# S5's parameter work beside the branch input products, and its gate tiles in two blocks instead of three

## The chip, the core and the metric

One core of a Trainium2 chip. The metric is the device time of one execution in microseconds, lower is better. Engines: TensorE (PE; PEld is its weight load), VectorE (DVE), ScalarE (ACT), GpSimd (POOL), and SyncE (SP), which here only issues DMA transfers.

## The reference

A first block (two layers of Fourier, pooling and latent attention) gives h; a second block, one layer, mixes four branches of 256 channels: S5, forgetting attention, RWKV and stick-breaking attention. Sequence 1024, width 1024. What the change touches is the S5 branch, a state space model of 16 groups with 16 channels and 64 complex states each:

```python
proj = h @ w_in[i]
(s5_u, fq, fk, fv, ff, rw, sq, sk, sv, gates) = _split(proj, IN_SPLIT_SIZES)
# _s5_mixer
dt = jnp.exp(log_dt)[:, None]
mag = jnp.exp(lam_re * dt); ang = lam_im * dt
lb_re = mag * jnp.cos(ang); lb_im = mag * jnp.sin(ang)
den = jnp.square(lam_re) + jnp.square(lam_im); nr = lb_re - 1.0
f_re = (nr * lam_re + lb_im * lam_im) / den
f_im = (lb_im * lam_re - nr * lam_im) / den
bb_re, bb_im = f * b          # complex product, per group
bu = ug @ bb                  # inputs of the states
x = associative_scan(x[t] = lb * x[t-1] + bu[t])
y = Re(c @ x) + d * ug
y = jax.nn.gelu(y); y = y * jax.nn.sigmoid(y @ glu_w + glu_b)
# later
merged = sum(sigmoid(gates[:, :, n]) * (branches[n] @ w_branch[i, n]) for n in range(4))
```

The gates are a part of the same projection: 4096 columns, 32 tiles of 128.

## The kernel before

Channels lie on the 128 partitions, positions along the free axis. A product in float32 is made from two parts of each operand (hi and lo), three products of fp32r matmuls: hi·hi, hi·lo, lo·hi. Weights come in tiles of 1024 x 128 (512 KB) through class `Weights`: `load` (SP, DMA into `w_raw`, two buffers; tile g waits for the split of tile g-2), `split` (GpSimd: a cast to `w_hi`, L197, and a subtract to `w_lo`, L201; waits for the end of tile g-2's products), and the products on TensorE.

**Branch input products** (`branch_products`, L608). 23 tiles (`N_PROJ2`) of the projection, 48 matmuls of 128x512 each, two PSUM accumulators in turn. VectorE reads each tile into `stage` times the row norm (L458, L460; L448 for the two S5 tiles, 8 and 9, which it writes by position within a chunk of 8), ScalarE's queue issues the store to `proj2` in HBM. For tiles 0 to 7 VectorE also norms a row of h.

**Gate tiles** (`GateTiles`, L673). They fill TensorE in the branches behind. A tile is two halves of 512 positions, 24 matmuls each (L696), with two PSUM banks once `gates.two` is set. VectorE reads each half into `gate_stage` (L723), SP stores it to `gates_kept` (L734, L736). A block says how many pieces (`gates.tensor(pe, n)`, 8 pieces to a half), reads, stores and splits it takes, at fixed places in each engine's program, which runs in order. Of a half, bank x may be begun when half x-2 was read; a read waits for the store of half x-2.

**S5** (`s5_branch`, L2493, and `s5_states`, L2783) has three parts in two blocks:
1. Parameters (6 gate tiles). SP loads the parameters, the masks, `glu`, and u from `proj2` in two layouts (2 rows and 16 rearranged pieces). VectorE makes dt, angles, coefficients, powers of lambda (`pw`), shift powers (`aw`) and the output matrices `hout`, in chains of small operations; ScalarE makes Exp and Sin; GpSimd clears `toe` and the pads of the scan and makes `fin` with six wide operations. The 12 gate reads stand between them.
2. States, in the same hardware block (6 gate tiles). TensorE transposes `fin`, makes the local states from u and the Toeplitz rows from `hout` and `bb`; SP spreads these into `toe` with 8 transfers; VectorE runs the scan over 128 chunks: 7 steps of 32 shifts (L2865) with a gate read after 16 of them; then TensorE has only gate halves.
3. Outputs, in a block of its own (2 gate tiles). TensorE: output products (L2740, L2742), 2 gate halves, wait for Gelu, GLU product (L2750), 2 gate halves. Between them results go to HBM and come back in another layout.

A hardware block ends when all engines are through; the row after it shows `PEq`, `POOLq` as what ended the wait. At each block's end SP clears the semaphores of the block before it. The RWKV branch follows.

Of the kernel before, what the change touches and what calls it, by code (L numbers as in the profile page):

```python
# [15 lines left out]

# [11 lines left out]
P = 128  # L28
# [584 lines left out]
def branch_products(core, io, hi, lo, stage, sq, h_all, vecs, r, ones, coming, comes_first):  # L613
# [6 lines left out]
    with core.phase(*x.SEMAPHORES, "stored0", "stored1", "h_normed", "h_stored", "next_in") as (block, *sems):  # L620
        stored0, stored1, h_normed, h_stored, next_in = sems[len(x.SEMAPHORES):]
# [757 lines left out]
def second_block(core, io, h_all, h_life, ones, ident, final_w, r, comes_first):  # L1379
# [3 lines left out]
    with core.scope():  # L1383
        vecs = core.sb("vecs2", [P, int(V_END)])
        right = ExitStack()
        with core.scope():
            h_at = 122880
            hi, lo = (rows_of(core.place("h2", [P, KT, T2], h_at + n * 4 * KT * T2, FR)) for n in range(2))
            with core.scope():
                stage, last_sq = core.sb("stage", [P, 2, T2]), core.sb("last_square", [P, TP])  # L1390
                branch_products(core, io, hi, lo, stage, last_sq[:], h_all, final_w, r, ones, [(vecs[:], io["vec2"])],
# [6 lines left out]
            with core.scope():  # L1398
                s5_branch(core, io, gates, masks, vecs, ybr, [(masks[:], io["masks"])])
# [1093 lines left out]
def s5_branch(core, io, gates, masks, vecs, ybr, coming):  # L2493
# [3 lines left out]
    nc = core.nc  # L2497
    par = core.sb("s5_par", [P, 3, 8])
    bc = core.sb("s5_bc", [P, 4, 8, S5_CH])
    tmp = core.sb("s5_tmp", [P, 16, 8])  # L2500
    rnd = core.sb("s5_round", [P, 8], I32)
    pw = core.sb("s5_powers", [P, 2, SC + 1, 8])
    aw = core.sb("s5_shift_powers", [P, 3, 7, 8])
    bb = core.sb("s5_bbar", [P, 3, 8, S5_CH])
    fin = core.sb("s5_in", [P, 2, 8, P])
    finT = ybr[:, BR_S5:BR_S5 + 2, :].rearrange("p a (t n) -> p a t n", t=8)
    hout = core.sb("s5_out", [P, 2, S5_G, (SC + 1) * S5_CH])
    toe = core.sb("s5_toeplitz", [P, S5_G, P])
    u = core.sb("s5_u", [P, 2, T2])
    ug = core.sb("s5_ug", [P, S5_G, NCH])  # L2510
    glu = core.sb("s5_glu", [P, 2, 2, P])
    ks = [ybr[:, 2 + 3 * n:5 + 3 * n, :].rearrange("p a t -> p (a t)")
          .rearrange("p (q t n) -> p q t n", q=2, t=8) for n in range(2)]
    kt = core.sb("s5_scan_tmp", [P, 2, 2, T2])
    lre, lim, ldt = (par[:, i, :] for i in range(3))
    (dt, mag, ang, turns, sn, sh, den, nr, fre, fim, t1, t2, t3, rdn, _, _) = (tmp[:, i, :] for i in range(16))
    PI = 3.1415925

    def cmul(tt, out_re, out_im, ar, ai, br, bi, p, q):

        tt(p, ar, br, ALU.mult)
# [6 lines left out]

    gates.two = True
    loads = 16 * (3 + len(coming) + 2 * SC)  # L2530
    with core.phase("p_dve", "p_exp", "p_ang", "p_sin", "p_ready", "p_pool", "p_out", "p_in", "par_in", "bc_in",
                    "rest_in") as \
            (block, stepped, exp_ready, ang_ready, sin_ready, par_ready, pool_step, hout_ready, fin_ready, par_in,
             bc_in, rest_in):
        @block.sync
        def _(sp):
            sp.dma_start(par[:], io["s5_par"]).then_inc(par_in, 16)
            sp.dma_start(bc[:], io["s5_bc"]).then_inc(bc_in, 16)
            sp.dma_start(glu[:], io["s5_glu_w"]).then_inc(rest_in, 16)
            for dst, source in coming:  # L2540
                sp.dma_start(dst, source).then_inc(rest_in, 16)
            for m in range(2):
                sp.dma_start(u[:, m, :], io["proj2"][P_S5 + m]).then_inc(rest_in, 16)
                for i in range(SC):
                    sp.dma_start(ug[S5_CH * i:S5_CH * (i + 1), 8 * m:8 * m + 8, :],
                                 io["proj2"][P_S5 + m].rearrange("(g c) (i n) -> i c g n", g=8, i=SC)[i]) \
                        .then_inc(rest_in, 16)
            gates.sync(sp, 6)

        @block.tensor  # L2550
        def _(pe):
            gates.tensor(pe, 12 * KT)

        @block.scalar
        def _(act):
            link = chain(act, exp_ready)
            act.wait_ge(par_in, 16)
            link(nc.scalar.activation(dt, ldt, ACT.Exp))
            act.wait_ge(ang_ready, 1)
            link(nc.scalar.activation(mag, mag, ACT.Exp))  # L2560
            nc.scalar.activation(sn, ang, ACT.Sin).then_inc(sin_ready, 1)
            nc.scalar.activation(sh, ang, ACT.Sin, scale=0.5).then_inc(sin_ready, 1)

        @block.vector
        def _(dve):
            link = chain(dve, stepped)

            def tt(o, a, b_, op):
                link(nc.vector.tensor_tensor(o, a, b_, op))

            def ts(o, a, s1, s2, op0, op1=ALU.bypass):
                link(nc.vector.tensor_scalar(o, a, s1, s2, op0, op1) if s2 is not None
                     else nc.vector.tensor_scalar(o, a, s1, None, op0))
            dve.wait_ge(exp_ready, 1)
            tt(mag, lre, dt, ALU.mult)
            tt(ang, lim, dt, ALU.mult)

            ts(turns, ang, 1.0 / (2 * np.pi), None, ALU.mult)
            link(nc.vector.tensor_copy(rnd[:], turns))
            link(nc.vector.tensor_copy(turns, rnd[:]))  # L2580
            for part in (6.28125, 0.0019350051879882812, 3.0199159819999247e-07):
                ts(t1, turns, part, None, ALU.mult)
                tt(ang, ang, t1, ALU.subtract)
            link(nc.vector.tensor_scalar(ang, ang, PI, -PI, ALU.min, ALU.max))
            nc.vector.tensor_copy(t1, ang).then_inc(ang_ready, 1)
            for _half in range(2):
                gates.vector(dve)
            dve.wait_ge(sin_ready, 2)
            dve.wait_ge(exp_ready, 2)
            tt(t1, sh, sh, ALU.mult)  # L2590
            ts(t1, t1, -2.0, 1.0, ALU.mult, ALU.add)
            lbr, lbi = pw[:, 0, 1, :], pw[:, 1, 1, :]
            tt(lbr, mag, t1, ALU.mult)
            tt(lbi, mag, sn, ALU.mult)
            tt(t1, lre, lre, ALU.mult)
            tt(t2, lim, lim, ALU.mult)
            tt(den, t1, t2, ALU.add)
            link(nc.vector.reciprocal(rdn, den))
            ts(nr, lbr, 1.0, None, ALU.subtract)
# [12 lines left out]
            dve.wait_ge(bc_in, 16)
            tt(bb[:, 0], wide(fre), bc[:, 0], ALU.mult)
            tt(bb[:, 2], wide(fim), bc[:, 1], ALU.mult)
            tt(bb[:, 0], bb[:, 0], bb[:, 2], ALU.subtract)
            tt(bb[:, 1], wide(fre), bc[:, 1], ALU.mult)
            tt(bb[:, 2], wide(fim), bc[:, 0], ALU.mult)
            tt(bb[:, 1], bb[:, 1], bb[:, 2], ALU.add)
            gates.vector(dve)

            link(nc.vector.memset(pw[:, 0, 0, :], 1.0))
# [1532 lines left out]
```

## Time and profile before

| | us |
|---|---|
| median of 3 runs | 3381.97 |
| lowest, highest | 3373.53, 3384.65 |
| span of the profiled execution | 3381.1 |

The profiled execution's device time isn't given apart from its span. The page of the profile shows TensorE busy for 95% of the span, VectorE for 61%, ScalarE 30%, GpSimd 29%. A timeline row gives start, duration, engine, line, operation, tiles and count; in brackets the idle time before it and what ended it. Ends of matmuls are modelled, so idle times of TensorE are a little short; starts are exact. A row of the waits says: engine and line, for whom it waited, total us, times, longest.

### The profile page before, as it was taken

Reading aid. Unit: us, or ns where it says so; the run is one execution under the profiler, and the core shown is the slowest. Engines: PE = TensorE matmul, PEld = TensorE weight load, DVE = VectorE, ACT = ScalarE, POOL = GpSimd, SP = SyncE. Lnnn points to the kernel's source line nnn. Section 1 sums busy time; section 2 is a strip of 40 time slices with the busy share of each in tenths; the row PEclk is TensorE's granted clock in tenths of the full one; section 3 lists DMA queues with packets and bytes.
Section 4 is the critical chain, followed back from the end, with each engine's and each line's share of the span. In section 5 each row is a group of like instructions: output and inputs, shape, how many; then the busy total and the mean of one; then the engine's idle time right before and its main releaser. Section 6 shows DMA issues by size and latency. Waiting matters only on the chain. (4 is left out here: it accounts for less than half of the span.)

```text
span 3381.1 us, 41800 instructions
## 1 busy us (share of the span) xinstructions
PE 3200.5 (95%) x17082; PEld 2723.7 (81%) x17082; DVE 2047.7 (61%) x2416; ACT 1009.5 (30%) x1456; POOL 967.0 (29%) x623
## 2 busy tenths in 40 slices
PE   7998999999899999998888999999999999999997
PEld 7997888999688898877767996666677787888875
DVE  5635664444466544118856554655686766896788
ACT  2113332101233320001022221455432644344644
POOL 3320001333000023334323322100132443445575
PEclk9999999999999999999989999999999999999998
DMA  3120000211100013233241002311261454355443
GB/s 134 44 64 9 21 1 19 77 44 44 33 29 1 7 45 143 101 104 95 83 146 57 1 1 92 86 44 35 97 237 58 140 180 160 119 189 170 149 158 120
DMA packets 111758, 282.12 MB, mean 83 GB/s; under 512 B 15010, under 2 KB 20770, under 8 KB 111552
## 3 DMA queue, kind: packets, MB, share of 16 engines
q1 hardware_dynamic: 107104, 263.19, 23.9%
q10 hardware_dynamic: 4464, 16.25, 1.2%
q8 instruction: 136, 2.23, 0.3%
q14 instruction: 54, 0.44, 0.0%
HBM read 237.37 MB, written 41.42 MB: 82 GB/s over the span
## 5 line engine op out<-in xcount | busy, mean ns | idle before, releaser
L197 POOL CAST w_hi<-w_raw 128x1024 fp32r<-128x1024 f32 x116 | 136.8, 1179 | 1780.7 <-PE psum L210 1112.6
L3595 PE MATMUL psum<-x,w_hi 128*128 128x512 f32 x2016 | 626.0, 392 | 8.3 <-DVE x L3566 3.2
L3595 PEld LDWEIGHTS psum<-x,w_hi 128*128 128x128 f32 x2016 | 378.4, 188 | 93.0 <-issue 6.9
L3595 PE MATMUL psum<-x,w_lo 128*128 128x512 f32 x1008 | 393.0, 390 | 0.0
L696 PE MATMUL psum<-h,w_hi 128*128 128x512 f32 x1024 | 331.8, 406 | 31.2 <-DVE gate_stage L723 17.8
L3480 POOL TENSOR_TENSOR w_lo<-w_sum,w_hi 128x512 fp32r<-128x512 f32 x180 | 251.9, 1407 | 331.2 <-ACT w_hi L3474 331.2
L201 POOL TENSOR_TENSOR w_lo<-w_raw,w_hi 128x1024 fp32r<-128x1024 f32 x116 | 302.8, 2610 | 16.4 <-DVE y L1501 7.2
L696 PEld LDWEIGHTS psum<-h,w_hi 128*128 128x128 f32 x1024 | 190.8, 193 | 83.5 <-issue 25.5
L3595 PEld LDWEIGHTS psum<-x,w_lo 128*128 128x128 f32 x1008 | 189.6, 188 | 39.6
L210 PE MATMUL psum<-hn_hi,w_hi 128*128 128x348 f32 x864 | 189.0, 327 | 17.7 <-DVE hn_lo L407 16.2
L696 PE MATMUL psum<-h,w_lo 128*128 128x512 f32 x512 | 203.6, 398 | 0.0
L210 PE MATMUL psum<-h,w_hi 128*128 128x512 f32 x736 | 197.0, 389 | 0.0
L210 PE MATMUL psum<-hn_hi,w_lo 128*128 128x348 f32 x864 | 184.9, 322 | 0.0
L210 PE MATMUL psum<-hn_lo,w_hi 128*128 128x348 f32 x864 | 184.8, 322 | 0.0
L3474 ACT ACTIVATE w_hi<-w_sum 128x512 fp32r<-128x512 f32 x180 | 112.3, 630 | 207.9 <-DVE w_sum L3462 207.8
L210 PEld LDWEIGHTS psum<-hn_hi,w_hi 128*128 128x128 f32 x864 | 147.2, 190 | 21.2 <-issue 13.6
L210 PEld LDWEIGHTS psum<-h,w_hi 128*128 128x128 f32 x736 | 138.1, 188 | 28.7
L1170 ACT ACTIVATE prob<-psum,softmax_small 116x1044 f32<-116x1044 f32 x72 | 81.4, 1131 | 226.2 <-DVE softmax_small L1219 226.2
L210 PEld LDWEIGHTS psum<-hn_lo,w_hi 128*128 128x128 f32 x864 | 146.9, 189 | 0.0
L210 PEld LDWEIGHTS psum<-hn_hi,w_lo 128*128 128x128 f32 x864 | 146.4, 189 | 0.0
L3462 DVE TENSOR_TENSOR w_sum<-w_raw 128x512 f32<-128x512 f32 x121 | 119.9, 994 | 29.5 <-PE psum L3595 23.2
L1136 PE MATMUL psum<-kept_slots,wqk 128*128 128x348 f32 x384 | 122.6, 467 | 11.0 <-DVE kn_lo L1251 7.8
(465 smaller groups left out, 6494.3 us busy)
## 6 DMA issues: line engine op xcount, KB each, us to landing
w_raw<-in_w_mlp SPq DMA_DIRECT2D x169, 256.0 KB, 2.9
norm_factor<-in_w_mlp SPq DMA_DIRECT2D x87, 256.0 KB, 2.8
w_raw<-in_w_mlp SPq DMA_DIRECT2D x42, 512.0 KB, 3.4
w_raw<-in_w_in SPq DMA_DIRECT2D x36, 512.0 KB, 3.5
w_raw<-in_w_gates SPq DMA_DIRECT2D x32, 512.0 KB, 3.9
gates_kept<-gate_stage SPq DMA_DIRECT2D x64, 256.0 KB, 2.1
gates<-gates_kept SPq DMA_DIRECT2D x32, 512.0 KB, 3.3
w_raw<-in_w_out SPq DMA_DIRECT2D x24, 512.0 KB, 3.5
```

The lines of the kernel that those rows point to most:

```text
L197: self.core.nc.gpsimd.tensor_copy(self.hi[:, g % 2], self.raw[:, g % 2]).then_inc(self.hi_done, 1)
L201: self.core.nc.gpsimd.tensor_tensor(self.lo[:, g % 2], self.raw[:, g % 2], self.hi[:, g % 2].bitcast(F32), ALU.subtract) \
L210: last = nc.tensor.matmul(acc[:, c, :], w[:, g % 2, k, :], x(k)[:, c * ch:(c + 1) * ch], start=(k == 0 and part == 0), stop=(k == kt - 1 a ...
L696: last = nc.tensor.matmul(self.core.psum[:, self.bank(x // KT), :], one[:, g % 2, k, :], other(k)[:, c * CH2:(c + 1) * CH2], start=(k == 0 ...
L1136: last = nc.tensor.matmul(bank(j), wqk[n % 2][:, k0 + k, cols], slots[:, src + k, chunk(c)], start=(k == 0), stop=(k == kt - 1))
L1170: nc.scalar.activation(prob[s % 2].rearrange("p (c n) -> p c n", c=3), scores, ACT.Exp, bias=nmx[:, s % 2:s % 2 + 1], scale=MLA_SCALE, acc ...
L3462: self.core.nc.vector.tensor_tensor(self.slot(self.core.weights.sums, j), raw[:, 0:4], raw[:, 4:8], self.SUMS[q]).then_inc(self.w_summed, 1)
L3474: self.core.nc.scalar.activation(self.slot(self.core.weights.hi, j), self.weight_source(j), ACT.Copy) \
L3480: self.core.nc.gpsimd.tensor_tensor(self.slot(w.lo, j), self.weight_source(j), self.slot(w.hi, j).bitcast(F32), ALU.subtract).then_inc(sel ...
L3595: last = self.core.nc.tensor.matmul(out, one[:, k, :], other[:, k, :], start=(group == 0 and k == 0 and part == 0), stop=(group == second ...
```

## The change

- A class `S5Inputs` holds S5's tensors at fixed places in SBUF, so that they live from the branch input products on.
- In `branch_products` SP loads the parameters after the first two weight tiles, and u (18 transfers) once tiles 8 and 9 are stored, ahead of the load of weight tile 14 of the stage. ScalarE does Exp ahead of tile 8's store and Exp and two Sin ahead of tile 10's. VectorE does, after its read of a tile: angle (tile 9), coefficients (11), powers (12), shift powers and the memset of `hout` (13), `hout` (14 to 17), `fin` (18, 19), the last on VectorE instead of GpSimd.
- The parameter part is gone. The states block begins with one gate tile on TensorE (2 reads, one store pair), GpSimd's clears stand at its start; behind the S5 products come 9 gate tiles instead of 6. In the scan a gate read stands after 32 shifts and then after every 12.
- The output block has 4 gate tiles instead of 2: 5 halves ahead of the GLU product, 3 behind it.
- 14 gate tiles in all, as before. The branch stage's block has 7 semaphores more; the S5 states block has 10 where the block before had 19.

```diff
@@ branch_products
-            x.sync(sp)
+            x.sync(sp, up_to=2)
+            sp.wait_ge(h_normed, 1)
+            s5.sync_parameters(sp, io)
+            x.sync(sp, up_to=P_ATT + 2, first=2)
+            for b in range(2):
+                sp.wait_ge(stored[b], 16 * (P_ATT // 2))
+            s5.sync_rows(sp, io)
+            x.sync(sp, first=P_ATT + 2)
             sp.wait_ge(next_in, 16 * len(coming))
+            s5.sync_end(sp)
...
             for m in range(N_PROJ2):
+                if m == KT:
+                    s5.scalar_step(act)
+                if m == KT + 2:
+                    s5.scalar_angle(act)
                 x.wait_read_out(act, m)
...
+                if m == KT + 1:
+                    s5.vector_angle(dve)
+                if m == KT + 3:
+                    s5.vector_coefficients(dve)
+                if m == KT + 4:
+                    s5.vector_powers(dve)
+                if m == KT + 5:
+                    s5.vector_shift_powers(dve)
+                if m in (KT + 6, KT + 7):
+                    s5.vector_out(dve, 0, SC, m - KT - 6)
+                if m in (KT + 8, KT + 9):
+                    s5.vector_out(dve, SC, SC + 1, m - KT - 8)
+                if m in (KT + 10, KT + 11):
+                    s5.vector_in(dve, m - KT - 10)
@@ S5Inputs (new)
+    def sync_rows(self, sp, io):
+        for m in range(2):
+            sp.dma_start(self.u[:, m, :], io["proj2"][P_S5 + m]).then_inc(self.u_in, 16)
+            for i in range(SC):
+                sp.dma_start(self.ug[S5_CH * i:S5_CH * (i + 1), 8 * m:8 * m + 8, :],
+                             io["proj2"][P_S5 + m].rearrange("(g c) (i n) -> i c g n", g=8, i=SC)[i]) \
+                    .then_inc(self.u_in, 16)
+    def scalar_angle(self, act):
+        nc, tmp = self.core.nc, self.tmp
+        act.wait_ge(self.ang_ready, 1)
+        nc.scalar.activation(tmp[:, 1, :], tmp[:, 1, :], ACT.Exp).then_inc(self.exp_ready, 1)
+        nc.scalar.activation(tmp[:, 4, :], tmp[:, 2, :], ACT.Sin).then_inc(self.sin_ready, 1)
+        nc.scalar.activation(tmp[:, 5, :], tmp[:, 2, :], ACT.Sin, scale=0.5).then_inc(self.sin_ready, 1)
+    def vector_in(self, dve, part):
+        tt, pw, bb, kt, fin = self.tt, self.pw, self.bb, self.kt, self.fin
...
+        tt(s1, pr, bi if part else br, ALU.mult)
+        tt(s2, pi, br if part else bi, ALU.mult)
+        tt(out, s1, s2, ALU.add if part else ALU.subtract)
@@ s5_branch: the parameter phase, removed (cut)
-            gates.sync(sp, 6)
...
-            gates.tensor(pe, 12 * KT)
...
-            gates.gpsimd(pool, 3)
-            pool.wait_ge(par_ready, 1)
@@ s5_branch, outputs
-            gates.sync(sp, 1)
+            gates.sync(sp, 2)
             for m in range(2):
                 sp.wait_ge(s5_done, m + 1)
                 sp.dma_start(io["s5_kept"][m], ybr[:, BR_S5 + m, :]).then_inc(s5_kept, 16)
-            gates.sync(sp, 1)
+            gates.sync(sp, 2)
...
-            gates.gpsimd(pool, 2)
+            gates.gpsimd(pool, 4)
...
-            gates.tensor(pe, 2 * KT)
+            gates.tensor(pe, 5 * KT)
             pe.wait_ge(gelu_ready, 2)
...
-            gates.tensor(pe, 2 * KT)
+            gates.tensor(pe, 3 * KT)
...
+            gates.vector(dve)
             for j in range(2):
                 dve.wait_ge(y_in[j], 16 * 8)
...
-            for _half in range(2):
+            for _half in range(4):
                 gates.vector(dve)
             for m in range(2):
                 dve.wait_ge(glu_ready, m + 1)
...
-            for _half in range(2):
+            for _half in range(3):
                 gates.vector(dve)
@@ s5_states
+            for dst, source in coming:
+                sp.dma_start(dst, source).then_inc(rest_in, 16)
+            gates.sync(sp, 1)
+            sp.wait_ge(cleared, 1)
             sp.wait_ge(g_saved, 4)
...
-            gates.sync(sp, 6)
+            gates.sync(sp, 9)
...
-            gates.gpsimd(pool, 6)
+            nc.gpsimd.memset(toe[:], 0.0).then_inc(cleared, 1)
+            for n in range(2):
+                nc.gpsimd.memset(ks[n][:, :, :, 0:KSPAD], 0.0).then_inc(cleared, 1)
+            gates.gpsimd(pool, 10)
...
-            pe.wait_ge(rest_in, loads)
-            pe.wait_ge(fin_ready, 1)
+            gates.tensor(pe, 2 * KT)
+            pe.wait_ge(rest_in, 16 * len(coming))
...
-            gates.tensor(pe, 12 * KT)
+            gates.tensor(pe, 18 * KT)
...
                 done[0] += 1
+                if done[0] > 20 and done[0] % 12 == 8:
+                    gates.vector(dve)
+            for _half in range(2):
+                gates.vector(dve)
+            dve.wait_ge(cleared, 3)
             dve.wait_ge(l_saved, 4)
...
-                if n >= 1:
-                    gates.vector(dve)
...
-                if n >= 2:
-                    gates.vector(dve)
             gates.vector(dve)
```

## Rows read from the trace of the kernel before

**Rows 1.** The page's first part: busy us, share, instructions.
```profile
PE 3200.5 (95%) x17082; PEld 2723.7 (81%) x17082; DVE 2047.7 (61%) x2416; ACT 1009.5 (30%) x1456; POOL 967.0 (29%) x623
```

**Rows 2.** Stretches: window, its length, PE, PEld, DVE, ACT, POOL busy, PEclk, DMA share, GB/s.
```profile
1272.00:1508.40 236.40, 236.35 (x1043) 195.38 (x1041) 51.50 (x30) 0.83 (x1) 73.72 (x43) 1.00 0.32 114
...
1512.70:1731.10 218.40, 193.81 (x928) 154.85 (x929) 158.89 (x377) 19.28 (x28) 79.95 (x38) 0.97 0.34 102
```

**Rows 3.** TensorE's waits from 1500 to 1735: total us, times, longest.
```profile
PE psum L696 <- DVE gate_stage L723: 12.6, 8, 2.4
...
PE psum L696 <- POOL w_lo L201: 1.3, 1, 1.3
```

**Rows 4.** Timeline of TensorE, where pieces of the S5 stage start.
```profile
1512.79 1.19 PE L696 MATMUL psum<-h,w_hi 128*128 128x512 f32 x2 [4.44 <-PEq L124]
...
1526.04 0.61 PE L696 MATMUL psum<-h,w_hi 128*128 128x512 f32 x2
...
1591.02 1.03 PE L2818 MATMUL psum<-masks,s_in 128*128 128x128 f32 x8
...
1604.12 0.74 PE L696 MATMUL psum<-h,w_hi 128*128 128x512 f32 x2
...
1609.73 0.61 PE L696 MATMUL psum<-h,w_hi 128*128 128x512 f32 x2
...
1615.17 0.61 PE L696 MATMUL psum<-h,w_hi 128*128 128x512 f32 x2
...
1681.97 0.77 PE L2740 MATMUL psum<-s_ug,s_toeplitz 128*128 128x128 f32 x2 [4.10 <-PEq L124]
...
1694.06 0.71 PE L696 MATMUL psum<-h,w_hi 128*128 128x512 f32 x2
...
1708.53 8.83 PE L2750 MATMUL psum<-s_scan_tmp,s_glu 128*128 128x512 f32 x16 [3.29 <-ACT s_scan_tmp L2763]
1716.80 1.03 PE L696 MATMUL psum<-h,w_hi 128*128 128x512 f32 x2
...
1731.11 0.70 PE L696 MATMUL psum<-h,w_hi 128*128 128x512 f32 x2 [2.86 <-PEq L124]
```

**Rows 5.** A stretch of the second block: the columns of rows 2.
```profile
1661.25:1664.00 2.75, 2.75 (x8) 2.16 (x7) 2.75 (x11) 0.00 (x0) 0.00 (x0) 0.50 0.55 182
```

**Rows 6.** Timeline of VectorE in the scan.
```profile
1639.70 4.28 DVE L2865 SCALAR_TENSOR_TENSOR branches<-branches,s_shift_powers 128x128 f32<-128x128 f32 x16
...
1651.11 0.68 DVE L723 TENSOR_TENSOR gate_stage<-psum,norm_factor 128x512 f32<-128x512 f32 x1
1651.71 7.27 DVE L2865 SCALAR_TENSOR_TENSOR branches<-branches,s_shift_powers 128x128 f32<-128x128 f32 x16
```

**Rows 7.** Timeline of GpSimd in the scan.
```profile
1616.43 4.43 POOL L197 CAST w_hi<-w_raw 128x1024 fp32r<-128x1024 f32 x1 [21.59 <-DMA w_raw<-in_w_gates]
1620.95 2.40 POOL L201 TENSOR_TENSOR w_lo<-w_raw,w_hi 128x1024 fp32r<-128x1024 f32 x1
...
1640.93 3.96 POOL L197 CAST w_hi<-w_raw 128x1024 fp32r<-128x1024 f32 x1 [10.38 <-PE psum L696]
...
1651.81 1.14 POOL L197 CAST w_hi<-w_raw 128x1024 fp32r<-128x1024 f32 x1 [4.45 <-PE psum L696]
```

**Rows 8.** SP's queue behind the Toeplitz products.
```profile
1604.84 6.81 SPq L2801 DMA_DIRECT2D s_toeplitz<-s_scan_tmp  x8
```

**Rows 9.** Stretches of the first S5 block: the columns of rows 2.
```profile
1512.70:1591.00 78.30, 69.42 (x288) 55.27 (x289) 64.18 (x125) 3.29 (x6) 43.81 (x21) 0.97 0.45 124
1546.11:1563.89 17.78, 16.16 (x70) 13.05 (x71) 15.29 (x48) 0.00 (x0) 3.48 (x2) 1.00 0.31 103
1564.54:1575.39 10.85, 8.39 (x36) 6.59 (x36) 10.68 (x7) 0.00 (x0) 10.63 (x5) 1.00 0.24 67
1576.00:1588.02 12.02, 10.56 (x47) 8.44 (x46) 11.86 (x6) 0.00 (x0) 11.78 (x5) 1.00 0.21 74
```

**Rows 10.** Timeline of VectorE in the branch input products; 14 tiles alike.
```profile
1388.78 1.22 DVE L458 TENSOR_TENSOR stage<-psum,norm_factor 128x1024 f32<-128x1024 f32 x1 [9.65 <-PE psum L210]
```

More of the change, by code:

```diff
@@ new lines, in vector_powers @@
+    def vector_powers(self, dve):
+        nc, tt, link, pw, kt = self.core.nc, self.tt, self.link, self.pw, self.kt
+        link(nc.vector.memset(pw[:, 0, 0, :], 1.0))
+        link(nc.vector.memset(pw[:, 1, 0, :], 0.0))
+        n = 1
+        while n < SC:
+            some, last = slice(1, n + 1), [pw[:, q, n, :].unsqueeze(1).broadcast_to([P, n, 8]) for q in range(2)]
+            s1, s2 = (kt[:, 0, q, 0:n * 8].rearrange("p (n t) -> p n t", t=8) for q in range(2))
+            p = self.cmul(None, pw[:, 1, n + 1:2 * n + 1, :], pw[:, 0, some, :], pw[:, 1, some, :], last[0], last[1],
+                          s1, s2)
+            link(nc.vector.tensor_copy(pw[:, 0, n + 1:2 * n + 1, :], p))
+            n *= 2
@@ new lines, in vector_shift_powers @@
+    def vector_shift_powers(self, dve):
+        nc, link, pw, aw = self.core.nc, self.link, self.pw, self.aw
+        t1, t2 = self.tmp[:, 10, :], self.tmp[:, 11, :]
+        link(nc.vector.tensor_copy(aw[:, 0:2, 0, :], pw[:, :, SC, :]))
+        for n in range(1, 7):
+            p = self.cmul(None, aw[:, 1, n, :], aw[:, 0, n - 1, :], aw[:, 1, n - 1, :], aw[:, 0, n - 1, :],
+                          aw[:, 1, n - 1, :], t1, t2)
+            link(nc.vector.tensor_copy(aw[:, 0, n, :], p))
+        link(nc.vector.tensor_scalar(aw[:, 2], aw[:, 1], -1.0, None, ALU.mult))
+        link(nc.vector.memset(self.hout[:], 0.0))
@@ new lines, in vector_out, with powers, coeff @@
+    def vector_out(self, dve, n0, n1, part):
+        nc, tt, link, pw, bc, kt, hout = self.core.nc, self.tt, self.link, self.pw, self.bc, self.kt, self.hout
+        w = n1 - n0
+        def powers(q):
+            return pw[:, q, n0:n1, :].rearrange("p n t -> p t n").unsqueeze(3).broadcast_to([P, 8, w, S5_CH])
+        def coeff(i):
+            return bc[:, i].unsqueeze(2).broadcast_to([P, 8, w, S5_CH])
+        a, c2 = (kt[:, 0, q, 0:8 * w * S5_CH].rearrange("p (t x) -> p t x", t=8) for q in range(2))
+        a4, c4 = (ap.rearrange("p t (n c) -> p t n c", n=w) for ap in (a, c2))
+        tt(a4, powers(part), coeff(2), ALU.mult)
+        tt(c4, powers(1 - part), coeff(3), ALU.mult)
+        for e in range(2):
+            rows = slice(64 * e, 64 * e + 64)
+            dst = hout[rows, part].rearrange("p (t e) n -> p t e n", e=2)[:, :, e, n0 * S5_CH:n1 * S5_CH]
+            if part == 0:
+                tt(dst, a[rows], c2[rows], ALU.subtract)
+            else:
+                link(nc.vector.scalar_tensor_tensor(out=dst, in0=a[rows], scalar=-1.0, in1=c2[rows],
+                                                    op0=ALU.mult, op1=ALU.subtract))
@@ new lines, in vector_in @@
+    def vector_in(self, dve, part):
+        tt, pw, bb, kt, fin = self.tt, self.pw, self.bb, self.kt, self.fin
+        pr, pi = (pw[:, q, SC - 1::-1, :].rearrange("p i t -> p t i").unsqueeze(3).broadcast_to([P, 8, SC, S5_CH])
+                  for q in range(2))
+        br, bi = (bb[:, q].unsqueeze(2).broadcast_to([P, 8, SC, S5_CH]) for q in range(2))
+        s1, s2, out = (ap.rearrange("p (t i c) -> p t i c", t=8, i=SC) for ap in (
+            kt[:, 1, 0, :], kt[:, 1, 1, :], flat(fin[:, part])))
+        tt(s1, pr, bi if part else br, ALU.mult)
+        tt(s2, pi, br if part else bi, ALU.mult)
+        tt(out, s1, s2, ALU.add if part else ALU.subtract)
@@ new lines, in s5_branch @@
+def s5_branch(core, io, gates, masks, vecs, ybr, inputs, coming):
+    nc = core.nc
+    x = inputs
+    u, kt, fin = x.u, x.kt, x.fin
+    toe = core.sb("s5_toeplitz", [P, S5_G, P])
+    glu = core.sb("s5_glu", [P, 2, 2, P])
+    assert nc.sbuf_base <= x.AT
+    finT = ybr[:, BR_S5:BR_S5 + 2, :].rearrange("p a (t n) -> p a t n", t=8)
+    ks = [ybr[:, 2 + 3 * n:5 + 3 * n, :].rearrange("p a t -> p (a t)")
+          .rearrange("p (q t n) -> p q t n", q=2, t=8) for n in range(2)]
+    gates.two = True
+    s5_states(core, io, gates, masks, x, finT, toe, ks, [(glu[:], io["s5_glu_w"])] + coming)
+    ug, hout = x.ug, x.hout
```

292 lines of the change are left out of this document (108 added, 184 removed).

## The prediction

> **What bounds the kernel now.** First the page's busy times: TensorE works in 3200.5 us of 3381.1, 95% [rows 1]. So a change that leaves TensorE's own work alone, as this one does (14 gate tiles, that is 28 halves of 24 matmuls, and the same S5 products), is worth what it takes out of TensorE's idle time. Then the stretches: in the branch input products TensorE is busy 236.35 of 236.40 us and VectorE only 51.5; in the S5 stage TensorE is busy 193.8 of 218.4 and VectorE 158.9 [rows 2]. The S5 stage has some 24 us to give, and the stage ahead has VectorE time free. Then what ended TensorE's waits in the S5 stage: 12.6 us in 8 waits for VectorE's read of a gate half, 1.3 for a weight split [rows 3], 3.29 for the Gelu [rows 4]. VectorE reads a half late because its instructions go in order, and S5's parameter work and scan stand ahead of the read. The idle time at three block borders (4.44, 4.10, and the one that ends at 1731.11, 2.86) stands in rows 4 too; it stays.
>
> **The S5 stage after the change, laid piece by piece.** It takes 1731.11 - 1512.79 = 218.3 us now. After, by the starts in rows 4:
> - first gate tile, with the slow start behind the border: 1512.79 to 1526.04, 13.25;
> - transposes, local states, Toeplitz products: 1591.02 to 1604.12, 13.1;
> - 18 gate halves at 5.44 (1609.73 to 1615.17), 97.9; border 4.1;
> - output products, 1681.97 to 1694.06, 12.1; 5 halves, 27.2; GLU product, 1708.53 to 1716.80, 8.3; 3 halves, 16.3; border 2.9.
>
> Sum 195.2. A half that starts behind something else takes 5.61 (1604.12 to 1609.73), 0.17 more, four times 0.7; 195.9. **Gain 22.4 us.** Where it lies: the first block's 78.2 us (1512.79 to 1591.02) hold 10.6 more than a tile of 13.25 and ten halves; the second's 73.8 (1604.12 to 1681.97 less 4.10) 8.5 more than twelve halves; Gelu 3.3. Of these 22.4, 17.2 are waits by name. 1.4 are the clock: from 1661.25 it is granted at 0.50 for 2.75 us [rows 5], against 1.00 in the branch stage [rows 2], 1.2 of 2.4 GHz, right behind a pause for VectorE. The rest is 0.4 for each of nine pauses (restart, and the modelled tail of the matmul before). I take 22.
>
> **Who must be in time for it.** (a) The scan. TensorE gives a tile each 10.88 us. VectorE's share of one is 24 shifts and two reads. 16 shifts take 4.28, so 24 take 6.4; a read takes 0.6 (1651.11 to 1651.71) [rows 6]: 7.6. But 16 shifts took 7.27 [rows 6] where GpSimd cast (1.14, from 1651.81) and subtracted (2.4 by its row at 1620.95) [rows 7]: 3.0 more, 10.6 in all. That is 0.3 under 10.88; with two banks a read may come a half, 5.4 us, late before TensorE stands, and the third read has only 32 shifts ahead of it, which begin before the Toeplitz products end. So it costs nothing; if the cover goes, about nine times the excess of a tile, less 5.4.
> By the Trainium skill (SBUF — State Buffer, Who interferes with whom) a VectorE instruction with two SBUF inputs and a GpSimd instruction that reads SBUF exclude each other for the whole instruction, and whoever comes first holds the other up. By that rule the trace agrees: 3.0 more beside a pair of 3.5; without it the tile would be put at 7.6, with it at 10.6.
> (b) SP's queue in the states block. The second next tile's weights are now loaded ahead of the eight Toeplitz transfers; the load behind them waits as before. They hold SP from 1604.84 for 6.8 us [rows 8]; those weights were in at 1616.43 and split by 1623.4 [rows 7], and their tile starts 21.8 us after 1604.12, at 1625.9. 2.5 us to spare, before and after. The 18 loads of u that filled SP at the stage's start, ahead of weights whose split came 1.3 late, are gone from there.
> (c) The last block. Gelu was ready 14.5 us after the output products (1708.53 - 1694.06); five halves give 27.2. Behind the GLU product SP waits for both S5 results before it stores the fifth half, whose buffer the seventh half's read wants. The product takes 8.3; sigmoid and multiply I put at 2.6 each, as the four wide operations of 10.2 us in rows 9 (next part), so the store goes out near 14, and the seventh half ends at 8.3 + 10.9 = 19.2. Nothing; 1 to 3 us if missed.
>
> **What is moved into the branch products.** VectorE is busy 64.2 us in the first S5 block, with 12 gate reads [rows 9]: 56 of parameter work. GpSimd's six operations come to it too: GpSimd was busy 43.8 us there [rows 9], of which six split pairs take at least 3.5 each; at most 23. Together 79. A tile's period is 10.88 with VectorE idle for 9.65 [rows 10]; 13 tiles hold 125. The fullest run: shift powers and memset, 17.8 us less two reads, 16.4 (tile 13); the wide output matrices, 10.9 and 12.0 us [rows 9] less a read each, 10.2 and 11.3 (tiles 14, 15). With 1.2 for the tile's own read VectorE gets late by 6.7, 7.2 and 8.8 us. TensorE stands only beyond 9.7 (a period less the read), as it has two accumulators. So even these prices cost nothing, and they are high: GpSimd was busy for 10.6 of 10.9 and 11.8 of 12.0 us beside them [rows 9], in the branch stage it is so for 73.7 of 236 [rows 2]. Bounds 0 and 3 us; I take 0.
> ScalarE: 3.3 us of moved work [rows 9]; its wait for VectorE's angle stands ahead of the issue of one tile's store, whose buffer is wanted two periods later. SP: the wait for the two stored tiles of u, then 18 issues, 15 us at the 0.85 of the Toeplitz ones (6.81 / 8, rows 8); behind them stand weight loads that have a tile's lead and more. GpSimd's split has a period, 10.88; the slowest rows give 4.43 + 2.40 = 6.8 [rows 7]. Nothing each. In the S5 stage GpSimd is only relieved.
>
> **Semaphores.** Seven more are cleared at the states block's end, nine fewer at the next. If the whole 1.2 us between those borders (4.10 and 2.86) is the 17 that the first clears more, that is 0.07 each: +0.5 and -0.7.
>
> **Behind the stage** the same tiles are left with the same loads and splits ahead, and blocks begin at borders, so the gain is carried to the end. No row speaks against it; 2 us either way.
>
> **Against the median.** The span, 3381.1, lies 0.9 below the median of 3382.0; its runs go from 3373.5 to 3384.7. Forecast 3382 - 22 = 3360.
>
> **Rivals.**
> 1. The lock makes the scan the bound, the page's rule at its worst. If cast and subtract cost VectorE 4.4 + 2.4 = 6.8, a tile takes 14.4, and nine tiles cost 9 x 3.5 - 5.4 = 26: 3386, no gain. Against it: the cast at 1640.93 took 3.96 while the 16 shifts from 1639.70 took their plain 4.28 [rows 6, 7], so a long cast is one that waits itself. 3%. Halfway, 12 a tile, costs 9 x 1.1 - 5.4 = 5: 3365, 7%.
> 2. Only part is freed: a read or a store is late somewhere (3 us of the branch bound, 3 of the last block) and the low clock comes once more, 1.4; gain 12 to 19, 3363 to 3370. 18%.
> 3. It doesn't do what it says: reads behind 12 shifts are as late as behind 16. The second block's 8.5 us on twelve halves become 12.7 on eighteen; gain under 10, 3373. 8%.
> 4. Slower: the weight split starves in the branch products behind VectorE's new two-input work. It decides where a pair takes longer than 10.88; each us beyond costs one on each of 11 tiles. Slower than before from 22 / 11 = 2 us beyond, a pair of 12.9, against the 6.8 of rows 7. A pair of 14 gives 3360 + 11 x 3.1 = 3394. VectorE has 125 us for 79, so it leaves gaps for GpSimd. 4%.
>
> The forecast, a gain of 19 to 25, has 60%.
>
> **How the numbers follow.** 0.3% is 10.1 us, about what a measurement of this kernel can tell from no change. Faster by more: 60 + 7 + 18, less 2 as medians spread: 83%. Within: rival 3, rival 1 at full price (3) and those 2, less 1 that may end slower: 12%. Slower: 4 + 1. The range: 3353 is a gain of 25 and 4 for the lower runs; 3374 is rival 2's end and 4 more, which takes in rival 3.
>
> **What would show it.** After: TensorE's first gate matmul to its first in the rwkv block 196 us apart; no wait for gate_stage above 0.5 us between them; no pause ahead of the GLU product; a granted clock of 1.00 between borders; VectorE some 115 to 130 us busy in the branch products with the tile's period still 10.88. Wrong if TensorE waits for a stage read or w_lo in the branch products, or VectorE has no idle time in the scan.

## The result

Four runs of the changed kernel have a median of 3360.8 us (3359.8 to 3361.8), four of the kernel before 3378.7 (3373.5 to 3384.7); the ratio is 0.9944, interval 0.9928 to 0.996. A second comparison, five runs of the changed kernel against nine, gave 3361.9 against 3380.5, 0.9944 (0.9931 to 0.9958). The profiled execution has a span of 3358.1 us against 3381.1, 23.0 less.

These are the stretches of the changed kernel, with the columns of [rows 2]: the branch input products, the S5 stage from its first gate matmul to the first of the RWKV block, and all behind it.

```profile
1272.00:1508.40 236.40, 236.23 (x1043) 195.22 (x1041) 113.87 (x157) 3.93 (x7) 76.86 (x43) 1.00 0.35 124
1512.67:1707.96 195.29, 188.09 (x929) 155.08 (x929) 105.70 (x257) 16.00 (x22) 51.77 (x32) 0.97 0.31 101
1707.96:3358.10 1650.14, 1577.20 (x7928) 1257.95 (x7928) 1148.40 (x1218) 661.33 (x983) 603.77 (x430) 0.98 0.33 112
```

The stage takes 195.3 us where it took 218.3 [rows 4]: 23.0, the whole difference of the spans. VectorE went from 51.5 to 113.9 us busy in the branch products and TensorE's 236.2 there didn't move. This is the same stretch of the kernel before, behind the stage:

```profile
1731.11:3381.10 1649.99, 1575.30 (x7928) 1256.78 (x7928) 1147.14 (x1218) 660.91 (x983) 606.77 (x430) 0.98 0.34 112
```

It took 1650.0 and takes 1650.1: the gain is carried to the end. This is what stopped TensorE from 1500 to 1712 in the changed kernel (line, for whom, total us, times, longest):

```profile
PE psum L727 <- PEq L126: 6.8, 2, 4.4
PE psum L2775 <- PEq L126: 4.6, 1, 4.6
PE psum L2862 <- ACT branches L2887: 0.3, 1, 0.3
```

Only three borders and 0.3 us at the transposes are left; the 12.6 for gate_stage and 1.3 for w_lo [rows 3] and the Gelu's 3.29 [rows 4] are gone. This is the scan on VectorE, one tile's worth and the start of the next:

```profile
1571.91 0.69 DVE L754 TENSOR_TENSOR gate_stage<-psum,norm_factor 128x512 f32<-128x512 f32 x1 [0.75 <-PE psum L727]
1572.52 5.78 DVE L2908 SCALAR_TENSOR_TENSOR branches<-branches,s_shift_powers 128x128 f32<-128x128 f32 x12
1578.22 0.69 DVE L754 TENSOR_TENSOR gate_stage<-psum,norm_factor 128x512 f32<-128x512 f32 x1
1578.82 3.24 DVE L2908 SCALAR_TENSOR_TENSOR branches<-branches,s_shift_powers 128x128 f32<-128x128 f32 x12
1582.80 0.69 DVE L754 TENSOR_TENSOR gate_stage<-psum,norm_factor 128x512 f32<-128x512 f32 x1 [0.74 <-PE psum L727]
```

and GpSimd beside it:

```profile
1572.01 1.04 POOL L199 CAST w_hi<-w_raw 128x1024 fp32r<-128x1024 f32 x1 [7.37 <-PE psum L727]
1573.13 2.39 POOL L203 TENSOR_TENSOR w_lo<-w_raw,w_hi 128x1024 fp32r<-128x1024 f32 x1
```

Twelve shifts take 3.24 alone and 5.78 beside a subtract of 2.39. A tile costs VectorE 10.1 us; now it is VectorE that waits, 0.75 us a tile. The fullest place in the branch products is on VectorE from the read of tile 13 on:

```profile
1410.41 1.23 DVE L462 SCALAR_TENSOR_TENSOR stage<-psum,norm_factor 128x1024 f32<-128x1024 f32 x1 [3.10 <-PE psum L212]
1411.55 2.40 DVE L2678 COPY s_shift_powers<-s_powers 128x16 f32<-128x16 f32 x1
...
1422.58 2.25 DVE L2591 TENSOR_TENSOR s_shift_powers<-s_shift_powers 128x8 f32<-128x8 f32 x1
...
1426.50 3.90 DVE L2684 MEMSET s_out<- 128x4608 f32 x1 [1.03 <-issue]
1430.43 1.23 DVE L460 TENSOR_TENSOR stage<-psum,norm_factor 128x1024 f32<-128x1024 f32 x1
1431.57 3.20 DVE L2591 TENSOR_TENSOR s_scan_tmp<-s_powers,s_bc 128x1024 f32<-128x1024 f32 x2
1434.80 4.56 DVE L2591 TENSOR_TENSOR s_out<-s_scan_tmp 64x1024 f32<-64x1024 f32 x2
1439.39 1.23 DVE L460 TENSOR_TENSOR stage<-psum,norm_factor 128x1024 f32<-128x1024 f32 x1
1440.53 2.48 DVE L2591 TENSOR_TENSOR s_scan_tmp<-s_powers,s_bc 128x1024 f32<-128x1024 f32 x2
1443.05 3.20 DVE L2705 SCALAR_TENSOR_TENSOR s_out<-s_scan_tmp 64x1024 f32<-64x1024 f32 x2
1446.28 1.23 DVE L462 SCALAR_TENSOR_TENSOR stage<-psum,norm_factor 128x1024 f32<-128x1024 f32 x1
```

With a period of 10.88 tile 14 was there at 1421.3 and is read at 1430.4, 9.1 late, where TensorE stands from 9.65 on. Tile 15 is 7.2 late, tile 16 3.2. The row at 1411.55 shows that GpSimd holds up more than two-input operations: it is a copy, which has one input, and it takes 2.40 us beside the subtract that GpSimd runs from 1411.53 to 1413.92; in the kernel before the same copy took 0.16 with GpSimd idle (1546.11).

### The profile page after: what moved, and what is told of

Read it like the earlier page. It is cut to its first block and busy times, and to the rows that moved or that the text cites. A ratio compares the mean times of both kernels' runs of the same rounds, so it can differ in the third digit from the quotient of the medians.

```text
span 3358.1 us, 41800 instructions
## 1 busy us (share of the span) xinstructions
PE 3196.7 (95%) x17082; PEld 2726.0 (81%) x17082; DVE 2058.2 (61%) x2422; ACT 1010.1 (30%) x1456; POOL 938.9 (28%) x617
## 5 line engine op out<-in xcount | busy, mean ns | idle before, releaser
L199 POOL CAST w_hi<-w_raw 128x1024 fp32r<-128x1024 f32 x116 | 126.2, 1088 | 1795.9 <-PE psum L212 1112.0
L203 POOL TENSOR_TENSOR w_lo<-w_raw,w_hi 128x1024 fp32r<-128x1024 f32 x116 | 301.9, 2602 | 16.4 <-DVE y L1533 7.2
```

The costliest lines, as they stand in the source:

```text
L199: self.core.nc.gpsimd.tensor_copy(self.hi[:, g % 2], self.raw[:, g % 2]).then_inc(self.hi_done, 1)
L203: self.core.nc.gpsimd.tensor_tensor(self.lo[:, g % 2], self.raw[:, g % 2], self.hi[:, g % 2].bitcast(F32), ALU.subtract) \
```

## Experiments: which part gives what

Runs differ by a few us ahead of and behind the stage (last section), so I compare the length of the stage, from its first gate matmul to the RWKV block's first. It is 195.3 in the changed kernel and 195.4 (1513.38 to 1708.76) in its second profile. Of that second profile this was expected:

> The changed kernel itself once more, against the kernel before. Theory: the S5 stage's 23 us are the whole gain; medians 3379 to 3381 before and 3358 to 3361 after, a gap of 18 to 23. Rival (the measured gap of 17.9 is real and 5 us are lost outside the stage): a gap of 16 to 18 again, and stretches outside the stage longer in the trace.

The medians are 3380.5 and 3361.9, a gap of 18.7. The S5 stage's 23 us are in both profiles of the changed kernel and the stretch behind is 1650.1 and 1651.3 against 1650.0. So nothing is lost there of a size that a profile shows. The gap of 18 to 19 between medians is less than the 23.0 between the spans. In every run that has both figures the time is 1.7 to 1.9 us above the span; by that, an estimate, the medians of the kernel before stand for spans of 3376.9 to 3378.7, and its one profile, 3381.1, lies 2.4 to 4.2 high. The first profile of the changed kernel, 3358.1, lies 0.9 low. That covers the difference; how much of it lies in the 218.3 us of the stage before, which only one profile shows, stays open.

**The work moved, the gate tiles left where they were.**

```diff
-            gates.sync(sp, 1)
+            gates.sync(sp, 6)
...
-            gates.tensor(pe, 2 * KT)
+            gates.tensor(pe, 12 * KT)
             pe.wait_ge(rest_in, 16 * len(coming))
...
-            gates.tensor(pe, 18 * KT)
+            gates.tensor(pe, 12 * KT)
...
-                if done[0] > 20 and done[0] % 12 == 8:
+                if done[0] in (48, 80, 96, 112, 128, 144, 160, 176, 192, 208, 224):
```

The output block has two tiles, as before; reads, stores and splits go with the tiles.

> The parameter work moved as in the changed kernel, but the gate tiles stay where they were: 6 ahead of the S5 products (VectorE has only reads there), 6 beside the scan with reads at the old places, 2 in the output block. Theory: only the 10.6 us of the first block are gained; the second block's 8.5 and the Gelu's 3.3 remain: span 3370 (3369 to 3371.5). Rival (moving the work is the whole gain): 3358 to 3360. Rival (placing is the whole gain): 3379 to 3381.

The median is 3368.6, the span 3367.1, 2 us below the range expected. TensorE's rows with a pause in the stage, without the 0.25 at the transposes and the border at 1672.74:

```profile
1513.75 1.19 PE L727 MATMUL psum<-h,w_hi 128*128 128x512 f32 x2 [4.45 <-PEq L126]
...
1618.23 0.70 PE L727 MATMUL psum<-h,w_hi 128*128 128x512 f32 x2 [1.57 <-DVE gate_stage L754]
1625.35 0.74 PE L727 MATMUL psum<-h,w_hi 128*128 128x512 f32 x2 [1.39 <-DVE gate_stage L754]
1642.25 0.70 PE L727 MATMUL psum<-h,w_hi 128*128 128x512 f32 x2 [0.24 <-DVE gate_stage L754]
1649.97 0.73 PE L727 MATMUL psum<-h,w_hi 128*128 128x512 f32 x2 [1.99 <-DVE gate_stage L754]
...
1700.44 7.13 PE L2785 MATMUL psum<-s_scan_tmp,s_glu 128*128 128x512 f32 x16 [2.99 <-ACT s_scan_tmp L2798]
1720.85 0.70 PE L727 MATMUL psum<-h,w_hi 128*128 128x512 f32 x2 [2.35 <-PEq L126]
```

The stage takes 207.1: moving alone gives 11.2 of the 23.0, where 10.6 were expected. The four pauses in the scan stand as they did, and the Gelu's is 2.99 where it was 3.29. The rest by which the span is below the one expected lies behind the stage (1646.3 against 1650.0), where nothing was edited.

**The gate tiles of the scan placed, those of the output block not.** Two of the output block's four tiles go back to the states block, behind the scan:

```diff
-            gates.tensor(pe, 18 * KT)
+            gates.tensor(pe, 22 * KT)
...
-            gates.tensor(pe, 5 * KT)
+            gates.tensor(pe, 2 * KT)
             pe.wait_ge(gelu_ready, 2)
...
-            gates.tensor(pe, 3 * KT)
+            gates.tensor(pe, 2 * KT)
```

The diff shows TensorE's part; reads, stores and splits go with it.

> The changed kernel, but the output block has its old 2 gate tiles (2 halves ahead of the GLU product, 2 behind it) and the states block 12 tiles instead of 10. Theory (each cover is worth what it hides): the Gelu wait of 3.3 us ahead of the GLU product comes back, nothing else; span 3358.1 + 3.5 = 3361.6. Rival (the gain came from the parameter work alone, the spread of gate tiles is worth nothing): span within 0.5 us of 3358.1.

The median is 3360.0, the span 3360.6. The stage takes 198.8 (1512.18 to 1710.98), with this one pause in it beside the borders and the 0.25 at the transposes (the view ends at 1690, so that it counts 3 of the product's 16 matmuls):

```profile
1688.89 1.55 PE L2785 MATMUL psum<-s_scan_tmp,s_glu 128*128 128x512 f32 x3 [2.99 <-ACT s_scan_tmp L2798]
```

That is 3.5 more than the changed kernel, as expected. In the median it can't be seen, with runs from 3357 to 3362. The three steps add up: 218.3, 207.1 (work moved), 198.8 (reads and tiles of the scan placed), 195.3 (output block).

**Reads after 16 shifts.**

```diff
-                if done[0] > 20 and done[0] % 12 == 8:
+                if done[0] > 32 and done[0] % 16 == 0:
```

The six halves left are read behind the scan.

> The changed kernel, but in the scan VectorE reads a gate half after 48 shifts, 80, and then every 16, instead of after 32 and then every 12; the six halves left are read behind the scan. Theory (VectorE's program order makes TensorE wait): a tile costs VectorE 32 x 0.267 + 1.2 + 2.5 for GpSimd's lock = 12.3 us against 10.88; the scan's 12 reads end some 6 us too late after the slack of one half, with restarts and perhaps a low clock 6 to 9 us: span 3364 to 3367, pauses of 1 to 2.5 us on gate_stage back in TensorE's rows. Rival (where the reads stand doesn't matter once the parameter work is gone): 3358, no pauses.

The median of ten runs is 3372.8 (3358.3 to 3375.0), the span 3368.1, 1 us above the range expected; the stage takes 202.4 (1510.92 to 1713.29), 7.1 more. The pauses are back (those at 1581.27 and 1605.88 are 0.29 each):

```profile
1588.98 0.73 PE L727 MATMUL psum<-h,w_hi 128*128 128x512 f32 x2 [2.02 <-DVE gate_stage L754]
...
1613.60 0.73 PE L727 MATMUL psum<-h,w_hi 128*128 128x512 f32 x2 [2.02 <-DVE gate_stage L754]
```

The four pauses are 4.6 us in all; the other 2.5 of the 7.1 are TensorE's busy time (190.6 against 188.1 us for the same 929 matmuls), with a granted clock of 0.96 over the stage where it was 0.97. So where the reads stand is a cause by itself. The median is 12 above the changed kernel's; of that the stage explains 7.1, and 4.7 more lie behind it in the profile (1654.8 against 1650.1), where nothing was edited.

This run also shows the long cast again, GpSimd's row and then VectorE's:

```profile
1570.24 3.99 POOL L199 CAST w_hi<-w_raw 128x1024 fp32r<-128x1024 f32 x1 [5.56 <-PE psum L727]
```
```profile
1573.24 0.68 DVE L754 TENSOR_TENSOR gate_stage<-psum,norm_factor 128x512 f32<-128x512 f32 x1
```

The cast ends at 1574.23, 1.0 us after VectorE's read of PSUM began, and a cast beside nothing takes 1.04. The one of 3.96 in rows 7 ends the same way, 1.0 us after a read that begins at 1643.90. So it waited for the read.

**The same with no subtract on GpSimd.** The memset in its place only writes SBUF; the low part of ten gate tiles' weights is left out. It stands in the states block alone.

```diff
-            self.core.nc.gpsimd.tensor_tensor(self.lo[:, g % 2], self.raw[:, g % 2],
-                                              self.hi[:, g % 2].bitcast(F32), ALU.subtract)
+            self.core.nc.gpsimd.memset(self.lo[:, g % 2].bitcast(F32), 0.0)
```

> As the run with reads at 16 shifts, but in the states block GpSimd writes zeros into w_lo with a memset instead of subtracting, so the low part of ten gate tiles' weights is left out of the result; TensorE does the same matmuls. Theory (the lock between a two-input VectorE instruction and a GpSimd instruction that reads SBUF costs VectorE 2.5 us a tile): VectorE needs 9.8 to 10.4 us a tile, under 10.88; the pauses go, span 3358 to 3359. Rival (VectorE is late by its own work): pauses and time as with reads at 16.

The median is 3356.1, the span 3353.8. The stage takes 195.4 (1510.06 to 1705.44), as in the changed kernel, and no wait for VectorE is left in it; that the span is 4 us lower comes from outside the stage. VectorE and, below, GpSimd:

```profile
1580.23 0.69 DVE L757 TENSOR_TENSOR gate_stage<-psum,norm_factor 128x512 f32<-128x512 f32 x1 [0.55 <-PE psum L730]
1580.83 4.63 DVE L2913 SCALAR_TENSOR_TENSOR branches<-branches,s_shift_powers 128x128 f32<-128x128 f32 x16
```
```profile
1580.33 1.04 POOL L199 CAST w_hi<-w_raw 128x1024 fp32r<-128x1024 f32 x1 [8.82 <-PE psum L730]
1581.43 0.96 POOL L204 MEMSET w_lo<- 128x1024 f32 x1
```

With reads at 16 and the subtract, the same 16 shifts took 6.7 or 7.3. Here they take 4.63 beside cast and memset and 4.3 alone. The 0.34 more is less than the memset's own 0.96, and it grows with the part of the cast that falls on the shifts: where the cast starts with them, at 1548.56, they take 5.07. So the memset costs VectorE nothing that can be told from the cast. The lock, and not VectorE's own work, makes the sixteen-shift pattern too slow. By the Trainium skill (SBUF — State Buffer, Who interferes with whom) only a GpSimd instruction that reads SBUF stands against a two-input VectorE instruction, one that only writes doesn't: the trace agrees, within that 0.34.

## Experiments: how much cover is left in the branch products

**The memset of s_out done twice, at tile 13.**

```diff
         link(nc.vector.memset(self.hout[:], 0.0))
+        link(nc.vector.memset(self.hout[:], 0.0))
```

> The changed kernel with the memset of s_out done twice (3.9 us more on VectorE behind the read of branch tile 13). In the changed kernel VectorE reads tile 14 at 1430.43, 9.1 us after the tile's end; TensorE could bear 9.65. Theory (the cover in the branch stage is all but used up at this tile): TensorE waits 3.4 us for the read of tile 14, once; span 3361.5 to 3362.5. Rival (there is slack that the periods don't show): span 3358, no wait in the branch stage.

The median is 3367.7, the span 3365.9: 7.8 more, twice what I expected. VectorE, then TensorE:

```profile
1426.04 3.90 DVE L2684 MEMSET s_out<- 128x4608 f32 x1 [1.03 <-issue]
1430.96 3.90 DVE L2685 MEMSET s_out<- 128x4608 f32 x1 [1.03 <-issue]
1434.90 1.23 DVE L460 TENSOR_TENSOR stage<-psum,norm_factor 128x1024 f32<-128x1024 f32 x1
```
```profile
1436.27 2.05 PE L212 MATMUL psum<-h,w_hi 128*128 128x512 f32 x4 [4.70 <-DVE stage L460]
1438.11 1.06 PE L212 MATMUL psum<-h,w_lo 128*128 128x512 f32 x2
1438.96 1.91 PE L212 MATMUL psum<-h,w_hi 128*128 128x512 f32 x4
```

The place and the mechanism are right: one wait, for the read of tile 14. I had left out the 1.03 us of issue ahead of a memset; 9.1 + 4.9 - 9.65 = 4.4, and 4.70 was measured. And I had left out the clock: behind the pause six matmuls take 2.69 us (1436.27 to 1438.96) and not 1.36, an eighth of the period. The stretch behind the pause, with the columns of [rows 2]:

```profile
1436.27:1441.50 5.23, 5.23 (x12) 4.15 (x13) 5.09 (x5) 0.00 (x0) 0.00 (x0) 0.50 0.52 195
```

The clock is granted at 0.50, the lower of its two levels (1.2 and 2.4 GHz), which costs half of these 5.2 us. The branch stage and its border last 247.5 us (1272.25 to 1519.73) against 240.0. In the changed kernel 0.5 us of lateness (9.65 less 9.1) was left before such a pause.

**More work still, at tile 20,** behind a read where VectorE had been idle.

```diff
+                if m == KT + 12:
+                    for _ in range(2):
+                        s5.link(nc.vector.memset(s5.kt[:], 0.0))
```

> The changed kernel with two memsets of s_scan_tmp (4096 wide, some 3.5 us and 1.03 of issue each, 9 us together) on VectorE behind the read of branch tile 20, where VectorE had 9.6 us idle. Theory (it is the place, not the sum of VectorE's work, that decides): no wait of TensorE in the branch stage, span within 1 us of the changed kernel's apart from the clock. Rival (more VectorE work in the stage costs wherever it is): 3 us or more, as one memset at tile 13 cost 7.5.

The median is 3355.5, the span 3352.7. VectorE there:

```profile
1485.59 3.47 DVE L702 MEMSET s_scan_tmp<- 128x4096 f32 x1 [0.80 <-issue]
1489.99 3.47 DVE L702 MEMSET s_scan_tmp<- 128x4096 f32 x1 [0.92 <-DVE s_scan_tmp L702]
1494.45 1.23 DVE L460 TENSOR_TENSOR stage<-psum,norm_factor 128x1024 f32<-128x1024 f32 x1 [0.99 <-PE psum L212]
```

It has 8.7 us of work more, with the idle 0.80 and 0.92 in it, and there is no wait of TensorE in the branch stage: its length with the border is 240.0 again (1269.67 to 1509.64), the S5 stage 194.8. That the whole run is 5 us shorter than the changed kernel isn't the memsets' doing: 3 us lie ahead of the branch stage, the rest behind. The place decides, not the sum: this work fits into the 9.6 us that VectorE had idle behind one read, so that no later read is late.

## Experiments: the borders

What is left is three borders, at the stage's start, between S5's blocks and at its end. The second went from 4.10 to 4.60 with 36 and 43 semaphores to clear, the third from 2.86 to 2.34 with 19 and 10.

**Clears at a block's start, on ScalarE**, instead of at its end on SP.

```diff
         with self.nc.Block() as block:
+            @block.scalar
+            def _(act):
+                for s in old_sems:
+                    act.sem_clear(s)
...
-            @block.sync
-            def _(sp):
-                for s in old_sems:
-                    sp.sem_clear(s)
```

> The changed kernel, but in every block the semaphores of the block before are cleared by ScalarE at the block's start instead of by SP at its end. Theory (a border's length is 1.5 us and 0.07 for each cleared semaphore: idle 4.10 for 36, 2.86 for 19 before; 4.60 for 43, 2.34 for 10 after): the border between S5's blocks goes from 4.60 to 1.6, the next from 2.34 to 1.6, all borders of the kernel together 5 to 10 us: span 3348 to 3353. Rival (the borders' length is the barrier and the last store): 3357 to 3359.

The median is 3348.6 (3345.9 to 3350.7), the ratio to the kernel before 0.9911 (0.9898 to 0.9924), the span 3348.5: the lowest median of this study. The second and third border:

```profile
1639.49 0.46 PE L2774 MATMUL psum<-s_ug,s_toeplitz 128*128 128x128 f32 x2 [1.56 <-PEq L126]
...
1702.62 0.70 PE L726 MATMUL psum<-h,w_hi 128*128 128x512 f32 x2 [1.72 <-PEq L126]
```

4.60 and 2.34 became 1.56 and 1.72, as expected. The stage takes 189.3, 6.0 less; 3.7 are the borders, the rest is that the low clock no longer stands behind the second (its first two matmuls took 0.77 in the changed kernel, 0.46 here). The border ahead of the stage stayed at 4.45, so clears aren't what ends it; what does isn't shown. All ten borders of the kernel took 25.5 us and take 20.4, which is 5.1 of the span's 9.6; the stretch behind the stage differs by as much between runs with nothing edited in it (last section). Whether the engine or the place of the clears matters was not told apart.

**States and outputs as one block.** TensorE waits by semaphores instead of at a border.

```diff
+    whole.enter_context(core.phase())
...
+            pe.wait_ge(g_saved, 4)
+            pe.wait_ge(toe_in, 16 * SC)
+            pe.wait_ge(dve_step, 32 * SHIFTS)
             for q in range(4):
```

> The changed kernel, but S5's states and outputs are one hardware block: TensorE waits by semaphores for toe_in, g_saved and the last shift instead of at a border. Theory: the border of 4.60 us and the low clock behind it (1.2 us) go; the border to the rwkv block clears 43 semaphores instead of 10 and takes 2.3 more: span 3358.1 - 5.9 + 2.3 = 3354.5. Rival (the border only showed a wait for the scan or the store): 3358.

The median is 3353.2, the ratio 0.9929 (0.9917 to 0.9942), the span 3350.6. The output products start with no pause at 1635.39; the border behind has 4.67 where it had 2.34. The stage takes 190.3 (1511.12 to 1701.39), 5.0 less against 3.6 expected: the low clock behind the border cost more than the 1.2 put down for it (TensorE is busy 185.4 us in the stage where it was 188.1).

**Both** edits in one kernel.

> Both: one S5 block, and the clears at the blocks' start on ScalarE. Theory: the clears' gain of the first of these runs, and 2.7 us more (a border of 1.5 and the low clock of 1.2 behind it): span 3345 to 3351. Rival: the two gains are the same time and don't add: as the better of the two.

The median is 3353.5 (3345.9 to 3355.9), the span 3351.8. The stage takes 187.4, the shortest (1513.82 to 1701.21): 1.9 less than with the clears alone, where 2.7 were expected. The two gains, 6.0 and 5.0, don't add even there: both take the same border and the low clock behind it, and with the clears moved only a border of 1.56 was left. But the stretch behind it, with the same instructions, takes longer than with the clears alone:

```profile
1701.21:3351.80 1650.59, 1577.15 (x7928) 1258.75 (x7928) 1145.06 (x1218) 661.10 (x983) 607.01 (x430) 0.98 0.33 112
```
```profile
1702.62:3348.50 1645.88, 1571.77 (x7928) 1255.27 (x7928) 1145.28 (x1218) 661.71 (x983) 607.78 (x430) 0.98 0.33 112
```

TensorE is busy 5.4 us longer for the same 7928 matmuls, so they ran at the low clock for longer. Why the clock falls more often there I can't say. In the time the one block adds nothing to the clears that these runs can tell; the lowest run of both kernels is 3345.9.

## Why the prediction was right

Forecast 3360, measured 3360.8. The places and the mechanism are as foreseen; that the figure agrees to 1 us is in part luck, as terms of the sum and the base were off in both directions.

- **The piecewise stage.** 195.9 us were laid from the starts in [rows 4], 195.3 came. The states border took 4.60 against 4.1 + 0.5, the last 2.34 against 2.9 - 0.7, and the GLU product starts without a pause. Two terms were wrong in opposite directions. The GLU product was laid at 8.3, which is its time behind the Gelu's pause, at a granted clock of 0.79 (1708.53 to 1716.80 in the kernel before); without the pause it took 6.5 (1682.23 to 1688.70). The output products were laid at 12.1 and took 13.2 (1641.76 to 1654.93), as the clock behind the border was granted at 0.51 up to 1647. The low clock behind the first two borders was rightly left in the sum; elsewhere the clock was 1.00 (1516 to 1637, 1648 to 1705). The pauses by name were ten and not nine (8, 1 and the Gelu's), 0.38 each for what lies around them; the sum of 22.4 doesn't hang on it.
- **Where the gain lay.** For the first block 10.6, for the scan 8.5 and for the Gelu 3.3 were foreseen; three kernels gave 11.2, 8.3 and 3.5. Rival 3 (reads behind 12 shifts are as late as behind 16) falls with the run at 16 shifts, rival 1 with the scan's rows: 10.1 a tile against the 10.6 forecast, since the lock costs 2.54 and not 3.0. The cast isn't stretched to 4 us any more: it now starts while VectorE reads PSUM, at 1572.01 in a row above. That a long cast is one that waits itself was right (run at 16 shifts).
- **Branch products.** TensorE not held up, as forecast, and the reasoning on the buffer (9.65 us late is the edge) holds to 0.3 us. But the terms beside it were off, in both directions. Shift powers and memset take 18.9 us (1411.55 to 1430.4) and not 16.4, as two pairs of GpSimd's splits fall on them and not one. The wide output matrices take 7.8 and 5.7 and not 10.2 and 11.3: those prices were taken beside a GpSimd that never paused. The greatest lateness was 9.1 at tile 14 and not 8.8 at tile 16, so the margin was near what was said, by luck of two errors. The moved work came to 62.4 us busy (113.9 - 51.5) against at most 79, and VectorE's 113.9 lie just under the 115 to 130 given as a sign.
- **Rival 4** (the split starves): GpSimd's busy time in the branch products went from 73.7 [rows 2] to 76.9, its slowest pair there took 5.4 of a period's 10.88 (1443.09 to 1448.51), and TensorE has no wait for w_lo.
- **SP.** The 18 loads of u took 9.3 us to issue and not 15, with nothing behind them late.
- **Against the median.** The change of the time was 18 to 19 us by medians and 23 by the trace; the forecast took 22 off a median of 3382 which four to nineteen runs put at 3378.7 to 3380.5. So the time was right and the gain by medians was over by 3 to 4: the base was too high by 1.5 to 3.3, which made up for most of it.

## What to carry to other kernels

Where an engine in program order both computes and frees another's buffers, write down per period what it must do between two such reads, with the lock of its neighbour in it, and spread the reads so that this is under the period; then ask how late one read may be. Move work to where that lateness has room, not to where the sum of idle time is: 8.7 us more were free at one tile and 4.9 cost 7.8 at another. At the end of a block count what the last engine still has to do: clears at its end cost 0.07 us each here (4.60 less 2.34 for 43 and 10 of them), and at its start on an idle engine nothing that TensorE's rows in the stage show.

## What the runs showed that I hadn't expected

A TensorE pause costs more than its length, and unevenly. Behind the same border of 4.45 us the first two gate matmuls take 1.19 us with the work moved alone (1513.75, above), as before [rows 4], and 0.70 with two memsets at tile 20:

```profile
1509.64 0.70 PE L730 MATMUL psum<-h,w_hi 128*128 128x512 f32 x2 [4.45 <-PEq L126]
```

In the latter the low clock comes about a microsecond later: it is granted at 0.63 from 1509.64 to 1512 and at 0.58 up to 1514. Pauses of 1.56 and 1.72 at the moved clears have none behind them. So after a pause of one length the low clock starts at different times in different runs. The stretch ahead of the branch products is the same code in all runs but the two with moved clears, and by the 240.0 us between them and the stage it ends between 1269.7 and 1273.8; the stretch behind the stage, with nothing of it edited, takes 1646.3 with the work moved alone and 1654.8 with reads at 16 shifts, TensorE 1574.7 and 1581.9 us busy in it for the same 7928 matmuls. These are the two:

```profile
1720.85:3367.10 1646.25, 1574.69 (x7928) 1257.45 (x7928) 1143.29 (x1218) 661.88 (x983) 603.40 (x430) 0.98 0.34 112
```
```profile
1713.29:3368.10 1654.81, 1581.94 (x7928) 1262.33 (x7928) 1140.71 (x1218) 661.84 (x983) 604.51 (x430) 0.98 0.34 111
```

The runs of one kernel lie up to 6 us apart (the changed one, nine runs) or 17 (the one before, nineteen runs), with no cause in its code, and an effect of 3 us is read from a stage in the trace, not from the time. What decides where in a run the clock falls stays open.
